# Chunk inverses corrected as 32x32 tiles, with the matmul units of a chunk step put in another order

## What is computed

```python
gcum = jnp.cumsum(gc, axis=-1)
decay = jnp.where(causal, jnp.exp(jnp.minimum(gcum[..., :, None] - gcum[..., None, :], 0.0)), 0.0)
kb = kc * bc[..., None]
lower = jnp.where(strict, jnp.einsum('nbhcd,nbhed->nbhce', kb, kc) * decay, 0.0)
tmat = lower + jnp.eye(A_CHUNK, dtype=f32)
rhs = jnp.concatenate([vc * bc[..., None], kb * jnp.exp(gcum)[..., None]], axis=-1)
sol = lax.linalg.triangular_solve(tmat, rhs, left_side=True, lower=True, unit_diagonal=True)
u, w = sol[..., :dv], sol[..., dv:]

def step(state, inp):                       # one chunk after another
    q_i, k_i, u_i, w_i, a_i, g_i = inp
    v_new = u_i - jnp.einsum('bhcd,bhdv->bhcv', w_i, state)
    o = (jnp.einsum('bhcd,bhdv->bhcv', q_i * jnp.exp(g_i)[..., None], state)
         + jnp.einsum('bhce,bhev->bhcv', a_i, v_new))
    g_last = g_i[..., -1]
    state = (state * jnp.exp(g_last)[..., None, None]
             + jnp.einsum('bhcd,bhcv->bhdv', k_i * jnp.exp(g_last[..., None] - g_i)[..., None], v_new))
    return state, o
```

## Time and profile before

| | us |
|---|---|
| median of 3 executions | 2419.62 (2416.2 to 2423.18) |
| the profiled execution, device time | 2413.46 |
| its span, first to last instruction | 2411.8 |
| tokens stage, 441 to 852 | 411 |
| delta stage, 986 to 1202 | 216 |
| PE busy over the span | 2253.9 (93%) |
| DVE busy over the span | 1405.0 (58%) |
| mean granted TensorE clock | 0.971 of full |

### The profile page before, as it was taken

One profiled execution on the slowest core, in us unless ns is written; L12 is line 12 of the kernel. 1 busy time (PEld: TensorE's weight loads), 2 busy tenths in 40 slices (PEclk: granted clock), 3 DMA queues, 4 the chain that ended last, 5 costly groups with the idle time before them and its releaser, 6 DMA issues. The chain is left out here.

```text
span 2411.8 us, 44567 instructions
## 1 busy us (share of the span) xinstructions
PE 2253.9 (93%) x18162; PEld 1994.9 (83%) x18162; DVE 1405.0 (58%) x1712; ACT 1069.8 (44%) x1581; POOL 549.3 (23%) x582
## 2 busy tenths in 40 slices
PE   6999999999999988877779999799999999999996
PEld 5777788999999976777735555799999999999995
DVE  5555311144564567344454468677777777777776
ACT  4666411011111167211255542466666666666664
POOL 1000000002876759444332210001000001000001
PEclk9999999999999999888889999899999999999998
DMA  3333422259888779699563322578777777877765
GB/s 125 87 96 91 143 85 103 101 132 272 223 251 234 201 212 289 168 226 220 157 228 127 127 88 114 219 268 266 266 276 268 256 257 274 267 262 266 266 227 207
DMA packets 274557, 479.04 MB, mean 199 GB/s; under 512 B 161456, under 2 KB 199472, under 8 KB 247248
## 3 DMA queue, kind: packets, MB, share of 16 engines
q1 hardware_dynamic: 239376, 420.82, 54.2%
q0 software_dynamic: 13856, 48.32, 7.1%
q10 hardware_dynamic: 21152, 7.48, 1.4%
HBM read 369.05 MB, written 111.42 MB: 199 GB/s over the span
## 5 line engine op out<-in xcount | busy, mean ns | idle before, releaser
L78 DVE TENSOR_TENSOR ex_w_rest<-weights,ex_w_rounded 128x2048 fp32r<-128x2048 f32 x192 | 439.4, 2290 | 204.1 <-ACT ex_w_rounded L2799 202.4
L2799 ACT CAST ex_w_rounded<-weights 128x2048 fp32r<-128x2048 f32 x192 | 365.6, 1905 | 12.7 <-PEq L48 12.7
L2691 PE MATMUL ex_g_acc<-ex_xt,ex_w_rounded 128*128 128x320 f32 x1024 | 271.3, 348 | 2.1 <-ACT ex_xt L2811 2.1
L2691 PE MATMUL ex_u_acc<-ex_xt,ex_w_rounded 128*128 128x320 f32 x1024 | 270.1, 347 | 0.0
L2692 PE MATMUL ex_g_acc<-ex_xt,ex_w_rest 128*128 128x160 f32 x1024 | 242.6, 237 | 0.0
L2692 PE MATMUL ex_u_acc<-ex_xt,ex_w_rest 128*128 128x160 f32 x1024 | 241.4, 236 | 0.0
L2692 PEld LDWEIGHTS ex_g_acc<-ex_xt,ex_w_rest 128*128 128x128 f32 x1024 | 197.0, 192 | 0.0
L2691 PEld LDWEIGHTS ex_g_acc<-ex_xt,ex_w_rounded 128*128 128x128 f32 x1024 | 193.7, 189 | 2.5 <-issue 2.5
L2692 PEld LDWEIGHTS ex_u_acc<-ex_xt,ex_w_rest 128*128 128x128 f32 x1024 | 195.4, 191 | 0.0
L2691 PEld LDWEIGHTS ex_u_acc<-ex_xt,ex_w_rounded 128*128 128x128 f32 x1024 | 192.0, 188 | 0.2
L2665 POOL DMA_INDIRECT x<-ex_ys,rt_sample_idx x15 | 24.5, 1634 | 638.8 <-issue 514.2
(11 more groups left out here) (420 smaller groups left out, 5260.0 us busy)
## 6 DMA issues: line engine op xcount, KB each, us to landing
weights<-in_w_expert SPq DMA_DIRECT2D x192, 1024.0 KB, 5.0
dl_la<-laq SPq DMA_DIRECT2D x40, 512.0 KB, 5.6
tk_w<-in_w_tok SPq DMA_DIRECT2D x10, 1344.0 KB, 7.4
ch_w<-in_w_ch SPq DMA_DIRECT2D x24, 512.0 KB, 5.2
sc_rows<-rows SPq DMA_DIRECT2D x40, 256.0 KB, 6.1
sc_qk<-qkv_ch SPq DMA_DIRECT2D x40, 256.0 KB, 6.2
laq<-sc_laq SPq DMA_DIRECT2D x20, 512.0 KB, 3.7
laq<-sc_laq SPq DMA_DIRECT2D x80, 128.0 KB, 3.7
```

The lines of the kernel that those rows point to most:

```text
L78: return dve.tensor_tensor(out, whole, rounded.bitcast(F32), ALU.subtract)
L2691: pe.matmul(bank[:, 0:2 * SLOTS], hi[:, cols], x.rearrange("p a n -> p (a n)"), start=first, stop=False, skip_group_check=True)
L2799: act.copy(w_hi[:, i % SPLIT], held[:, i % HELD]).then_inc(w_rounded, 1)
```

## The change

It has four parts.

1. In the tokens stage, LT is no longer stored. DVE writes the negated diagonal blocks (four operations of 32 partitions) into `diag` and the one negated off-diagonal block of each direction into `off` (two operations). They take the place of one 128x512 and two 128x256 operations. SP stores AT alone of the first pair, and `off` beside `diag`.
2. In the delta stage, `across` and `correction` work on raw 32x32 blocks: `off` times the inverse block `x0` that it needs, and the product times the other inverse `x1`. The rows are FAR (0 to 31 and 96 to 127) and NEAR (32 to 63 and 64 to 95). The 64x64 form `x`, the mask and POOL's operation for `x` go. `masked` and `transposed` become two copies each, of 32 partitions and 256 elements.
3. The units stand in another order on PE and DVE, `uobank` has two buffers (four banks instead of two), and `vbank` and `sbank` share two banks (`vsbank`). `from_state(s)` now waits for the output copies of step s-2.
4. The loads are split by use (`at`, `kq`, `off`, `x0`, `x1`, `kv`) and issued at other points of the step: 1536 KB for a step instead of 1792 KB, with the outputs 1792 KB instead of 2048 KB.

```diff
@@ phase_tokens, DVE @@
-                    dve.tensor_tensor(laq[:, b, 0], prod[:, b, :, CH:], laq[:, b, 0], ALU.mult).then_inc(lt_done, 1)
...
-                    dve.tensor_scalar(diag[:, b], blocks[:, :, 0, :], own[:, 0:1], None, ALU.mult).then_inc(diag_step, 1)
-                    for k in range(1, CH // BLK):
-                        dve.wait_ge(diag_step, done + k)
-                        last = dve.scalar_tensor_tensor(out=diag[:, b], in0=blocks[:, :, k, :], scalar=own[:, k:k + 1], in1=diag[:, b], op0=ALU.mult, op1=ALU.add)
...
+                    def block(out, rows, k):
+                        cols = slice(BLK * k, BLK * k + BLK)
+                        return dve.scalar_tensor_tensor(out=out[rows, b], in0=prod[rows, b, :, CH + cols.start:CH + cols.stop], scalar=-1.0, in1=laq[rows, b, 0, :, cols],
+                                                        op0=ALU.mult, op1=ALU.mult)
+                    for d in range(2):
+                        for k in range(CH // BLK):
+                            block(diag, slice(CH * d + BLK * k, CH * d + BLK * k + BLK), k)
+                    block(off, FAR[0], 1)
+                    block(off, FAR[1], 0).then_inc(lt_done, 1)
@@ phase_delta, SP, step p loads s = p + 3 @@
+                        sp.wait_ge(kq_done, p + 1)
+                        sp.wait_ge(lx_done, p + 1)
+                        load_across(sp, dr, off[b], x0[b], loaded[b], s)
                         sp.wait_ge(lx_done, p + 2)
+                        tokens(s, 0)
+                        sp.wait_ge(v_done, p + 1)
+                        tokens(s, 1)
+                        sp.wait_ge(corrected, p + 2)
+                        load_keys_queries(sp, dr, kq[b], loaded[b], s)
+                        sp.wait_ge(kd_done, p + 1)
+                        if p >= 1:
+                            sp.wait_ge(at_done, p)
+                        load_attended(sp, dr, at[b], loaded[b], s)
@@ phase_delta, PE @@
                 def from_state(s, b):
...
                         pe.wait_ge(state_out, s)
-                        pe.wait_ge(o_out, 2 * s)
+                    if not early(s, 2):
+                        pe.wait_ge(o_out, 2 * s - 2)
...
+                def across(s, b, i):
+                    pe.wait_ge(loaded[b], 16 * LOADS * (i + 1))
+                    if not early(s, 1):
+                        pe.wait_ge(prod_out, 2 * s)
+                    passed(s)
+                    for h in range(NH):
+                        for d in range(2):
+                            mm = pe.matmul(ybank[NEAR[d], d, 0, h, :], off[b][FAR[d], h, :], x0[b][FAR[d], h, :], start=True, stop=True)
+                    mm.then_inc(lx_done, 1)
...
+                def correction(s, b):
+                    pe.wait_ge(prod_out, 2 * s + 2)
                     if not early(s, 1):
+                        pe.wait_ge(xt_out, 2 * s)
                     passed(s)
+                    for h in range(NH):
+                        for d in range(2):
+                            mm = pe.matmul(ybank[FAR[d], d, 1, h, :], prod[NEAR[d], h, :], x1[b][NEAR[d], h, :], start=True, stop=True)
+                    mm.then_inc(corrected, 1)
...
                     from_state(s, b)
+                    if more:
+                        across(s + 1, nb, ni)
                     solve(s, b)
                     if more:
-                        across(s + 1, nb, ni)
+                        correction(s + 1, nb)
                     to_state(s, b)
                     to_output(s, b)
-                    if more:
-                        correction(s + 1, nb)
@@ phase_delta, DVE @@
                 def masked(s, b):
                     dve.wait_ge(lx_done, s + 1)
                     if not early(s, 1):
                         dve.wait_ge(corrected, s)
-                    dve.tensor_tensor(paired(prod[:]), narrow(ybank), below, ALU.mult).then_inc(prod_out, 1)
+                    for d in range(2):
+                        dve.tensor_copy(prod[NEAR[d]], ybank[NEAR[d], d, 0]).then_inc(prod_out, 1)
...
-                    dve.tensor_tensor(paired(xt[:, b]), narrow(ybank), paired(xt[:, b]), ALU.add).then_inc(xt_out, 1)
+                    for d in range(2):
+                        dve.tensor_copy(xt[FAR[d], b, :, BLK * (1 - d):BLK * (1 - d) + BLK], ybank[FAR[d], d, 1]).then_inc(xt_out, 1)
...
                     remainder(s, b)
+                    if more:
+                        masked(s + 1, nb)
                     keep(s, b)
                     if more:
-                        masked(s + 1, nb)
+                        transposed(s + 1, nb)
                     else:
                         first_tile.statistics(dve)
                     carried(s, b)
-                    if more:
-                        transposed(s + 1, nb)
```

More of the change, by code:

```diff
@@ L1490 @@
 class EarlyLoads:
-    la: list
-    blk: list
+    at: list
+    kq: list
+    off: list
+    x0: list
+    x1: list
     kv: list
     cols: object
-    masks: tuple
+    spread: object
     const_in: object
     loaded: list
-    CONSTANTS = 16 * 5
+    CONSTANTS = 16 * 4
     def start(self, engine, io, dr, s):
         if s == 0:
-            for dst, name in zip(self.masks, ("mask32", "spread")):
-                engine.dma_start(dst[:], io[name]).then_inc(self.const_in, 16)
+            engine.dma_start(self.spread[:], io["spread"]).then_inc(self.const_in, 16)
             load_columns(engine, dr, self.cols, self.const_in)
+        load_across(engine, dr, self.off[s], self.x0[s], self.loaded[s], s)
+        load_inverse(engine, dr, self.x1[s], self.loaded[s], s)
         for d in range(2):
-            load_blocks(engine, dr, self.blk[s], self.loaded[s], s, form=d)
             load_tokens(engine, dr, self.kv[s], self.loaded[s], s, d)
-        for pair in range(2):
-            load_factors(engine, dr, self.la[s], self.loaded[s], s, pair)
+        load_keys_queries(engine, dr, self.kq[s], self.loaded[s], s)
+        load_attended(engine, dr, self.at[s], self.loaded[s], s)
 def early_loads(nc, ctx):
@@ L1586, in _ @@
+                    load_tokens(sp, dr, kv[s % RING], loaded[s % RING], s, d)
                 for s in range(LOADED_EARLY, AHEAD_STEPS):
+                    load_across(sp, dr, off[s], x0[s], loaded[s], s)
+                    load_inverse(sp, dr, x1[s], loaded[s], s)
                     for d in range(2):
-                        blocks(s, form=d)
                         tokens(s, d)
-                    for pair in range(2):
-                        factors(s, pair)
+                    load_keys_queries(sp, dr, kq[s], loaded[s], s)
@@ L1657, in product @@
                                 h = 4 * ((wave + d) % 2) + n
[L1658 removed]
+                                mm = pe.matmul(bank[rows, h // 4, n, :], lhs[rows, h, :], moving[rows, h, :], start=True, stop=True)
                     mm.then_inc(done, 1)
@@ L1744, in step @@
                         half = slice(HD * (1 - d), HD * (1 - d) + HD)
-                        act.copy(ostage[half, b % 2], uobank[half, d]).then_inc(o_out, 1)
+                        act.copy(ostage[half, b % 2], uobank[half, b % 2, d]).then_inc(o_out, 1)
                     act.wait_ge(o_out, 2 * s + 2)
```

163 lines of the change are left out of this document (63 added, 100 removed).

## The result

The changed kernel takes 2391.49 us (median of 4 executions, 2387.24 to 2395.81), the kernel before, beside it, 2418.29 (2416.2 to 2423.18). The ratio is 0.9879, 95% interval [0.9861, 0.9897]: faster by 27 us, where 43 were forecast. The time lies inside the range (2366 to 2400), in the stretch that the first rival had (2388 to 2393), and outside the forecast's own range (2368 to 2384).

What follows compares the result with a forecast made beforehand. PE bounds the tokens stage, a ring of waits the delta stage. Sixteen steps of 8.0 and three of 7.7 us instead of 10.2 give -43 us: 2413.46 becomes 2370.5, forecast median 2376 (own range 2368 to 2384); range 2366 to 2400.

Steps and rivals of the forecast that it cites:

- the first rival: Delta stage: clock still falls or loads land late; 2388 to 2393 if partly, 2400 in full; chance 0.30 (2384 to 2402).
- The ring: Delta step's chain of waits, `from_state` to the next: 10.2 us before, 7.5 after at full clock, 7.7 with `correction`.
- The drain where the shape changes: Around `correction`, between `solve` and `to_state`: changing tile shape twice drains PE, upper end 7.8 instead of 7.5 us.
- "+0.2" for `correction`: Delta step: `correction` frees PE later than 5.5 us, by 0 to 0.3; 0.2 taken, making the period 7.7.
- "DMA and PE are about level, and I take 8.0 for 16 steps": Delta stage: 1.97 MB a step takes 8.0 us at 247 GB/s, 7.0 at 282; last 3 steps 7.7.
- "Only some 0.8 us idle": Delta step: `across` now precedes `solve`, leaving PE little idle; `solve` at 1.15 in nearly all steps, clock above 0.95.
- "I cost it at nothing; PE's matmuls hide it": Tokens stage: DVE's new operations add at most 1.4 us a step, 28 over the stage, hidden behind PE.
- The sum: First `dl_v` copy 998.07 plus 16 x 8.0 + 3 x 7.7 gives last copy 1149.2 against 1191.98: -43 us.
- Landing: Delta loads: a set lands at 14.2 to 16.5 us of step s, before `across` needs it at 17.4.
- No change: Rival: the end is set elsewhere, such as first tile's loads at step 17; within 0.3% (7 us), chance 0.05.
- Slower: Rival: PE stays at 1.2 GHz all through the delta step, 12.2 us a step, +38 us, 2458; chance 0.05.

Runs made afterwards that it cites:

- The filler: Three identity matmuls (0.85 us) put between `across` and `solve` in each delta step of the changed kernel: 2382.02 us, ratio 0.9847 to the kernel before.
- the wide one: Changed kernel with one 256-column identity matmul ahead of `solve` and the `off` stores issued by ACT: 2378.78 us, ratio 0.982 to the kernel before.
- its own control: Changed kernel with the stores of `off` issued by ACT instead of SP, no added matmul: 2386.88 us, ratio 0.9864 to the kernel before.

## Why the prediction was right, and where it was not

- **The ring: right.** The forecast's 7.5 to 7.7 for a step is 7.58. The units stand where it put them: `solve` starts 3.55 behind `from_state` (3.6), `to_state` 5.46 (5.5), the state operation 6.65 (6.65). The drain where the shape changes stayed what the earlier trace rows show: the tile unit starts 0.08 ahead of `solve`'s end (1073.69 against 1073.77). The tile unit takes 0.69 (0.74 taken), and "+0.2" for `correction` was 0, since it ends while ACT still copies. Putting either part back alone costs 16 to 18 us (order) or 30 us (bank), most of it through the clock: at full clock those steps are 7.93 and 8.78.
- **"DMA and PE are about level, and I take 8.0 for 16 steps": wrong, 7.1 us too long** (151.1 - 144.0). The 247 GB/s came from dividing a rate by a share. Steps of 7.58 ran at 269 to 283 GB/s with shares of 1.00 to 1.02, and no load held PE in them. So DMA is about level, as forecast, but at another rate: the busy share was no measure of what the engines can still move, and the row at 282 was the better guide.
- **"Only some 0.8 us idle", so the clock holds in nearly all steps: wrong.** Idle was 0.92, and nine of the 20 `solve` took 1.78 to 1.98. The first rival's mechanism is therefore partly true, in its clock half; its load half is not (0.3 us). The filler gets back 3.9 us of the copies' span in the profiles, and the wide one 8 to 11 us of the whole against its own control. I had priced it at 0.30 and did not let it into the forecast, although the loss at 0.92 idle had no row on either side: the earlier trace rows show a fall behind 1.58 and the earlier trace rows none behind 1.60, and nothing showed that less is safe.
- **Stops of PE while its code comes: not in the sum at all.** 2.0 us in the first step of the change; up to 3.7 in its variants. The kernel before had no stop of this kind above 0.5 from 1003 on, so no row warned of it. In the change the two stops are 2.4 of the 19.4 us; the larger part is the clock, with stops or without.
- **"I cost it at nothing; PE's matmuls hide it": off by 5.8 us.** DVE's new operations are indeed hidden (224.33 busy of 411, against 202.25, within the 28 us that I bounded). I had counted DVE's side alone and not SP's two more stores in front of the loads of `sc_qk`, for which PE waits. 2.4 of the 5.8 are a longer wait and some 3.0 the clock that fell behind it, as above; how much of the wait is the stores' is open. The stretch behind it gave a little back: the first `dl_v` copy is 4.3 late.
- **The sum.** -7.1 for steps of 7.58 in place of 8.0 and 7.7, +19.4 for clock and stops, +4.3 for the late start: 16.6, which is 1165.82 against the forecast 1149.2. The first term went the other way and made the miss smaller by luck. The direction and the ring were right by their mechanism; the size is right only by the width that the first rival gave to the range.
- **Landing: right.** `across` waited once for a load, 0.3 us. **No change: wrong**, and the tail is as before. **Slower: wrong.** A step of the rival's kind came once, in the variant with one bank's wait back, and that kernel as a whole is level with the kernel before (ratio 1.0002), not at 2458.

Open: why the clock holds in one step and falls in the next behind the same 0.92 us (1080.19 against 1087.78), and what share SP's stores have in the tokens stage.

## What to carry to other kernels

When a ring of waits is cut shorter, two things bound it: the buffer that lets the next turn start, and the unit that stands under each wait. Give both; here either one alone left 16 to 30 us lying. Then look at what stays idle ahead of the critical unit and put a matmul of no use there: it took 0.70 us of free PE time and kept the unit after it at full clock in all steps but two, both behind a stop. A new order can gain more by the clock than by the path: the old one lost 0.35 us a step at full clock and 2.7 with the clock down. When an engine's work is split into smaller pieces, count the issues it adds to every queue, not only the engine's own operations; here their price could not be told from a wait that came without them too.

## What the runs showed of the hardware that was not expected

- The granted clock fell behind 0.92 us of idle PE ahead of `solve` and held behind the same wait in other steps. With 0.29 us idle it held for eight steps in a row. In the old order it held in some steps behind 1.55 us, and in the tokens stage it held behind a wait of 2.52 us and fell behind one of 3.56.
- A unit of 32 records with 32x32 tiles takes 0.69 at 2.4 GHz and 1.06 at 1.2 GHz; the same count with 64x64 tiles 1.15 and 1.97.
- PE stopped for 0.4 to 8.75 us inside a unit or ahead of one, without a semaphore, in or beside stretches in which instruction packets moved on q8; with a filler, eight undisturbed steps followed where none moved. Behind stops of 3.68 and 8.75 the clock was down, so that `from_state` took 3.68 instead of 2.00.
- An issue of one small store on SP lasted from 0.57 to 3.51 us within the same step.
